# Cross attention's first two score steps, the output tiles and the first two pages' parts, each moved to an earlier place in a hybrid decoder step

## What is computed

```python
x = x + mix_output(o_gla, r, o_mla, lp)                    # w_out
x = x + cross_attend(rms_norm(x, lp['g_x']), mk, mv, lp)
x = x + ffn(rms_norm(x, lp['g_ff']), lp)

# latent attention of the prompt: causal softmax over the prompt's own keys, 8 heads
s = jnp.einsum('bthd,bshd->bhts', qn, kn) + jnp.einsum('bthd,bsd->bhts', qp, kp)
# latent attention of the samples: over 16 pages of 128 latent rows for each sequence
ckv = pool_ckv[pages]; kp = pool_kpe[pages]
kn, v = mla_decompress(ckv, lp)
# cross attention
q = rms_norm((h @ lp['w_xq']).reshape(B, T, X_HEADS, X_DIM), lp['g_xq'])
s = jnp.einsum('bthd,bnhd->bhtn', q, mk) * (X_DIM ** -0.5)
```

## Time and profile before

| | |
|---|---|
| median of 3 timed runs | 1205.99 us (1205.42 to 1207.26) |
| profiled execution, time | 1202.8 us |
| profiled execution, span | 1201.0 us |
| PE busy | 1153.9 us (96%) |
| VectorE, ScalarE, GpSimd busy | 607.1, 367.1, 310.3 us |
| mean granted clock of PE | 0.987 of full speed |
| read from memory | 107.90 MB |

### The profile page before, as it was taken

The page is one execution under the profiler, slowest core; times in us unless marked ns, Lnnn a source line. Parts: engine busy times, 40 slices in busy tenths (PEclk is TensorE's granted clock), DMA queues, the critical chain, the costliest instruction groups (busy, mean ns, idle before and its releaser), DMA issues.

```text
span 1201.0 us, 21983 instructions
## 1 busy us (share of the span) xinstructions
PE 1153.9 (96%) x8064; PEld 1022.8 (85%) x8064; DVE 607.1 (51%) x1062; ACT 367.1 (31%) x855; POOL 310.3 (26%) x180
## 2 busy tenths in 40 slices
PE   7999999989879999999989998999999999999997
PEld 4799896667869999999867764799999999999996
DVE  0659553767456677666621154444454444443442
ACT  4221124445444455545401143333310003330000
POOL 0127032720275777776602100300000000000000
PEclk9999999989999999999999999999999999999999
DMA  8432102100484444444126230222222222222102
GB/s 333 166 106 79 49 1 63 36 19 1 124 270 114 121 124 127 137 134 129 41 80 235 70 106 1 87 90 88 73 85 88 72 86 89 74 84 88 53 0 79
DMA packets 61601, 114.18 MB, mean 95 GB/s; under 512 B 6577, under 2 KB 41554, under 8 KB 61458
## 3 DMA queue, kind: packets, MB, share of 16 engines
q1 hardware_dynamic: 60946, 111.33, 29.7%
q0 software_dynamic: 576, 1.84, 0.4%
HBM read 107.90 MB, written 5.25 MB: 94 GB/s over the span
## 4 chain that ended last, share of the span: by engine, by line
PE 85%; DVE 4%; SPq 3%; issue 2%; POOL 2%; ACT 2%; DMA 2%; POOLq 0%; DVEq 0%; ACTq 0%
PE bank L1321 34%; PE bank L719 8%; PE bank L781 6%; PE bank L1133 5%; PE bank L1135 4%; PE bank L1134 4%; PE bank L799 3%; PE bank L743 2%; PE bank L1089 2%; PE bank L1160 2%; PE bank L1043 2%; PE bank L961 1%; SPq L629 1%; PE bank L1141 1%; PE bank L1063 1%
## 5 line engine op out<-in xcount | busy, mean ns | idle before, releaser
L1321 PE MATMUL bank<-hr,wr 128*128 128x288 f32 x1536 | 205.2, 296 | 1.0 <-DVEq L2295 1.0
L1321 PEld LDWEIGHTS bank<-hr,wr 128*128 128x128 f32 x1536 | 204.9, 189 | 1.4 <-issue 1.4
L1321 PE MATMUL bank<-ur,wr 128*128 128x288 f32 x1536 | 205.3, 296 | 0.0
L1321 PEld LDWEIGHTS bank<-ur,wr 128*128 128x128 f32 x1536 | 205.0, 189 | 0.1
L2609 POOL TENSOR_TENSOR stat<-stat,cst 128x32 f32<-128x32 f32 x32 | 175.2, 5476 | 2.5
L1133 PE MATMUL bank<-wq_high,c_parts 128*128 128x288 f32 x512 | 158.0, 309 | 2.6 <-DVE c_parts L2164 2.6
L1135 PE MATMUL bank<-wq_low,c_parts 128*128 128x288 f32 x512 | 152.6, 298 | 0.0
L1134 PE MATMUL bank<-wq_high,c_parts 128*128 128x288 f32 x512 | 151.7, 296 | 0.0
L2399 DVE CAST wr<-ring 128x1024 fp32r<-128x1024 f32 x64 | 44.4, 694 | 209.0 <-PE bank L1321 208.3
L2172 DVE TENSOR_REDUCE stat<-hT 128x8 f32<-128x512 f32 x128 | 86.6, 682 | 63.7 <-ACT hT L1633 61.7
L1133 PEld LDWEIGHTS bank<-wq_high,c_parts 128*128 128x128 f32 x512 | 97.3, 190 | 9.6 <-issue 8.4
(11 more groups left out here) (395 smaller groups left out, 1797.6 us busy)
## 6 DMA issues: line engine op xcount, KB each, us to landing
ring<-in_ring_w_dram SPq DMA_DIRECT2D x106, 512.0 KB, 3.6
arena<-in_page_rows_dram SPq DMA_DIRECT2D x128, 144.0 KB, 2.3
arena<-in_ckv_t_dram SPq DMA_DIRECT2D x96, 128.0 KB, 2.1
hT<-in_ckv_t_dram SPq DMA_DIRECT2D x32, 128.0 KB, 2.1
arena<-in_mk_t_dram SPq DMA_DIRECT2D x8, 512.0 KB, 3.2
arena<-in_cache_mv_dram SPq DMA_DIRECT2D x8, 512.0 KB, 10.2
mixT<-in_x_dram SPq DMA_DIRECT2D x1, 2048.0 KB, 12.9
out_dram<-hT SPq DMA_DIRECT2D x4, 512.0 KB, 3.2
```

The source lines that it names most:

```text
L1321: ins = mm(outs[c][:, 0:HALF], w[:, ew, k, :], src[:, ex, k0 + k, c * HALF:(c + 1) * HALF], start=(start and k == 0 and n == 0), stop=(sto ...
```

## The change

Four things are moved; no arithmetic is added or taken away.

1. In the query products PE does the third `value_rows` and the second `absorbed` before it waits for `q_ready` and `q_nope`, and `TURNED_ORDER`, ScalarE and VectorE follow this order.
2. The parts of the first pair of pages are made inside the prompt's attention: ScalarE's `high_parts(0, 0)` behind the third-last product with the values, VectorE's `turned(0, 0)` at the end of its steps. The buffer of the second pair of pages lies in `hT` now (column 512, over the second slot of `pr`), and SP loads this pair as soon as that slot has been turned the last time. PE no longer waits for the other engines at `phase_end`; it waits for the four banks of the page products, and for `page_one` only behind the first sequence.
3. SP issues the eight `W_OUT` tiles behind the first pair of pages, when `turned` is 4, and no longer behind the first `stream`.
4. In cross attention the first two score steps of the prompt stand behind the third query product, ahead of the fourth; the squares of the fourth query and the second roots come two steps later in the loop, and the banks of `cs` and `cp` are others.

```diff
     *(("kT", h) for h in range(4, MH)), ("vp", 0), "qTs", *(("kT", h) for h in range(4)), ("vp", 1), ("qabs", 0),
-    ("qT", 0), ("qT", 1), ("vp", 2), ("qabs", 1), ("qT", 2), ("qT", 3), ("qT", 4), ("qT", 5), "qpd", ("vp", 3),
+    ("vp", 2), ("qabs", 1), ("qT", 0), ("qT", 1), ("qT", 2), ("qT", 3), ("qT", 4), ("qT", 5), "qpd", ("vp", 3),
...
+    for b in range(2, 6):
+        fills[("page", b)] = (b, base[b])
...
-        fill(("cs", n % 4, n // 4), 1 + n % 2)
-        fill(("cp", n % 4, n // 4), 3 + n % 2)
+        fill(("cs", n % 4, n // 4), 2 + n % 2)
+        fill(("cp", n % 4, n // 4), (4, 1)[n % 2])
...
-        pages_t = [view(hT, 4096, 2, KC, P)] + [view(arena, c0, 2, KC, P) for c0 in (15908, 16420, 16932)]
+        pages_t = [view(hT, c0, 2, KC, P) for c0 in (4096, 512)] + [view(arena, c0, 2, KC, P) for c0 in (16420, 16932)]
...
 # SP
             sp.wait_ge(S("turned"), 4)
             load_pair(0, 0, 0)
+            for n in range(W_OUT, W_XQ):
+                load_tile(n)
+            b, n = PLAN[("pT", 3, MH - 3)]
+            sp.wait_ge(bank_full[b], n)
+            load_pair(0, 0, 1)
             sp.wait_ge(S("phase_end"), MET[3])
-            for n in range(1, 4):
+            for n in range(2, 4):
                 load_pair(0, 0, n)
             stream(0, 0, first=True)
-            for n in range(W_OUT, W_XQ):
-                load_tile(n)
...
 # PE
             absorbed(0)
+            value_rows(2)
+            absorbed(1)
             pe.wait_ge(S("q_ready"), TILES)
             pe.wait_ge(S("q_nope"), TILES)
-            for h in range(2):
-                turned_queries(h)
-            value_rows(2)
-            absorbed(1)
-            for h in range(2, 6):
+            for h in range(6):
                 turned_queries(h)
...
-            meet(pe, 3)
+            pe.drain().then_inc(S("phase_end"), 1)
...
+            for b in range(2, 6):
+                pe.wait_ge(bank_free[b], PLAN[("page", b)][1])
+            sequence(0, 0, first=True)
             pe.wait_ge(S("page_one"), 2)
-            sequence(0, 0, first=True)
...
                 project(("xq", j), lambda k: ring[:, s, k, :], hTk, KD, name=None if j else "x")
                 if j == 2:
                     query_squares(0)
+                    prompt_scores(0)
+                    prompt_scores(1)
...
-            for n in range(len(pairs) + 3):
+            for n in range(2, len(pairs) + 3):
                 if n < len(pairs):
-                    t, u = pairs[n]
...
+                    prompt_scores(n)
-                if n == 1:
+                if n == 3:
                     query_squares(1)
                 if n >= 3:
                     sample_scores(n - 3)
...
 # ScalarE
             for n in range(len(steps) + 5):
+                if n == len(steps) + 2:
+                    act.wait_ge(S("prT_used"), 4 * (MH // 2 - 1))
+                    high_parts(0, 0)
...
             def sequence(b, par, first=False, last=False):
-                if first:
-                    high_parts(b, 0)
...
+            for j in range(XH - 1):
+                query_squares(j)
...
                 if n == 1:
+                    query_squares(XH - 1)
+                if n == 3:
                     query_roots(1)
...
 # VectorE
             absorbed(0)
+            absorbed(1)
             turned_queries(1)
-            absorbed(1)
...
+            turned(0, 0)
             meet(dve, 3)
...
-                    if n in (0, 3):
-                        query_roots(n // 3)
+                    if n in (0, 4):
+                        query_roots(n // 4)
...
+                if n == 1:
+                    gained_queries(XH - 1)
```

More of the change, by code:

```diff
@@ L1209, in query_squares, with prompt_scores @@
                 filled(ins, ("ms_xq", u))
+            pairs = [(t, u) for u in range(2) for t in range(4)]
+            def prompt_scores(n):
+                t, u = pairs[n]
+                pe.wait_ge(S("xq"), 4 * u + 4)
+                o = reopen(pe, ("cs", t, u))
+                for e in range(2):
+                    h = 2 * u + e
+                    ins = mm(o[:, e * NM:(e + 1) * NM], xqT[:, h, t * P:(t + 1) * P], kmT[:, :, h, :],
+                             start=True, stop=True)
+                filled(ins, ("cs", t, u))
             for j in range(XH):
@@ L1215, in _ @@
                     query_squares(0)
-            pairs = [(t, u) for u in range(2) for t in range(4)]
+                    prompt_scores(0)
+                    prompt_scores(1)
             def sample_scores(q):
@@ L1590, in _, with high_parts @@
             arrive(act)
+            def high_parts(b, n):
+                act.wait_ge(S(f"page_t{n % 4}"), b * 128 + 64 * (n // 4 + 1))
+                if not (isinstance(b, int) and b == 0 and n < 2):
+                    act.wait_ge(S("kr"), b * NPG + (2 * n - 2))
+                nc.scalar.copy(c_parts[:, n % 2, 0, :, :, :].rearrange("p e k c -> p (e k c)"),
+                               pages_t[n % 4].rearrange("p e k c -> p (e k c)")).then_inc(S("c_high"), 1)
             steps = [(t, h) for t in range(4) for h in range(MH)]
             for n in range(len(steps) + 5):
+                if n == len(steps) + 2:
+                    act.wait_ge(S("prT_used"), 4 * (MH // 2 - 1))
+                    high_parts(0, 0)
                 if 3 <= n < len(steps) + 3 and (n - 3) % 2 == 1:
@@ L1634, in page_out @@
                   ACT.Square).then_inc(S("kr_free"), 1)
-            def high_parts(b, n):
-                act.wait_ge(S(f"page_t{n % 4}"), b * 128 + 64 * (n // 4 + 1))
-                if not (isinstance(b, int) and b == 0 and n < 2):
-                    act.wait_ge(S("kr"), b * NPG + (2 * n - 2))
-                nc.scalar.copy(c_parts[:, n % 2, 0, :, :, :].rearrange("p e k c -> p (e k c)"),
-                               pages_t[n % 4].rearrange("p e k c -> p (e k c)")).then_inc(S("c_high"), 1)
             def rope_keys(b, u):
@@ L1687, in _, with query_squares @@
                   scale=(EPS * XD / D) ** 0.5).then_inc(S("squares"), 1)
-            for j in range(XH):
+            def query_squares(j):
                 for c in range(2):
@@ L2129, in _, with turned @@
             dve.wait_ge(S("q_ready"), TILES)
+            def turned(b, n):
+                dve.wait_ge(S("c_high"), b * 8 + (n + 1))
+                V.tensor_tensor(c_parts[:, n % 2, 1, :, :, :].rearrange("p e k c -> p (e k c)"),
+                                pages_t[n % 4].rearrange("p e k c -> p (e k c)"),
+                                c_parts[:, n % 2, 0, :, :, :].rearrange("p e k c -> p (e k c)"),
+                                ALU.subtract).then_inc(S("c_low"), 1)
             steps = [(t, h) for t in range(4) for h in range(MH)]
@@ L2159, in _ @@
                 dve.nop().then_inc(S("sc_room"), 1)
-            def turned(b, n):
-                dve.wait_ge(S("c_high"), b * 8 + (n + 1))
-                V.tensor_tensor(c_parts[:, n % 2, 1, :, :, :].rearrange("p e k c -> p (e k c)"),
-                                pages_t[n % 4].rearrange("p e k c -> p (e k c)"),
-                                c_parts[:, n % 2, 0, :, :, :].rearrange("p e k c -> p (e k c)"),
-                                ALU.subtract).then_inc(S("c_low"), 1)
             def page_sums(b, j):
@@ L2247, in sequence @@
             def sequence(b, par, first=False, last=False):
-                if first:
-                    turned(b, 0)
                 for n in range(8):
@@ L2315, in _, with gained_queries @@
             add_to_x("wo", "x_mix", [(j, 0) for j in range(4)] + [(j, 1) for j in range(4)] + in_turn[8:], gained)
-            for j in range(XH):
+            def gained_queries(j):
                 for c in range(2):
@@ L2322, in _ @@
                     dve.wait_ge(S("xq"), n)
+            for j in range(XH - 1):
+                gained_queries(j)
             def query_roots(u):
```

9 lines of the change are left out of this document (1 added, 8 removed).

## The result

The changed kernel takes 1186.68 us (median of four runs, 1183.99 to 1190.21) against 1206.03 us before: a ratio of 0.984, with a 95% interval of 0.9813 to 0.9867. A later set of five runs gave 1188.82 us (1184.67 to 1190.79) against 1205.26 us, a ratio of 0.9871 (0.985 to 0.9892). The forecast was 1188.3 us.

The account below looks back on a forecast made before the run. The prediction took the matrix engine (PE), 85% of the chain, as the bound, through its waits and half-clock stretches. 5.62 + 3.36 + 8.35 + 0.4 = 17.7 us off the 1205.99 us median gave 1188.3 us, range 1185 to 1193.

Parts of the forecast that it names:

- Place A: Query products: a value and an absorbed product fill PE's 3.13 us wait, and the half clock behind it goes; gain 5.62 us.
- Place B: Hand-over from the prompt's attention to the pages: early parts and second pair put everything behind one pair earlier; gain 3.36 us.
- Place C: Output tiles: second sequence's pages no longer stand behind them on SP's queue; gain 8.35 us, bounds 6.66 to 8.35.
- Place D: Cross attention: two of ScalarE's steps run beside the fourth query product; gain 0.4 us, bounds -1.80 to 4.16.
- Rival 1: Clock falls at the hand-over and cross attention loses 1.80 us instead of winning 0.4: 1191.6 us; chance 0.20.
- Rivals 2 and 3: 2: half of Place C stays, 1192.5 us, chance 0.06; 3: most of Place B fails, A keeps half clock, 1194.2, 0.05.
- Rival 4: Attention: tiles hold six instruction transfers, 4.8 us each; attention 29 us longer, kernel at 1217 us; chance 0.03.

## Why the prediction was right

**Place A** was forecast at 5.62 us, its upper bound, and measured a little above it, at 5.80 and 5.74. The mechanism, idle time plus the half clock behind it, held; nobody held PE at the banks. The size is that of the one execution from which it was read. Over the four profiled executions with the old order the stage took 17.46 to 18.71 us, 17.99 on the mean, over the ten with the new order 12.95: the wait cost the same each time, the half clock behind it 1.4 to 2.6 us, and place A is worth 5.0 us on the mean.

**Place B** was forecast at 3.36 us and measured at 3.39 and 3.44. PE's first page product came 0.98 us after its last attention product, where some 0.7 us had been said, and the last release was the output copy, as said. One statement was off without touching the sum: PE was to wait for the third pair's transfer, and it reached the pair with less than 0.1 us to spare. The start itself was right: 309.93 is 8.61 us behind the start of the last product with the values, where the second pair had been 8.67 us behind. The early cast cost nothing: it ran while PE's last turning still did, the copy behind it starts 0.69 us after that turning (300.59 and 299.90), and PE waits 0.77 us for the copy, both as before.

**Place C** was forecast at 8.35 us. By the same spacing it measured 18.63 - 10.54 = 8.09 us. The spacing was read 0.26 us too small: 10.28 us had been taken one sequence on, and the second sequence keeps 10.54 us, of which 0.20 us is PE's wait for ScalarE ahead of `weighted`. By the whole stage it was 8.54 and 8.43 us, and 8.17 us alone. Here too the wait that goes is not a constant: the four profiled executions with all tiles at the old place had 6.66, 4.62, 6.37 and 7.61 us. Their stage took 49.41 us on the mean, the nine with all tiles early 40.91: 8.5 us. With four tiles the wait of 1.36 us follows from the bytes.

**Place D** was forecast at 0.4 us within -1.80 and 4.16. Eleven executions give 0.3 us on the mean, and 0.6 to 0.7 us at equal clock. The queue order that was to give most of the gain back did so, step by step: the second turning behind the sums of squares, then the roots, then VectorE. The run with the late second pair shows it, whose granted clock was 1.00 from there to 712 us: counted from the stage's start, ScalarE's fourth, fifth and sixth steps came 2.05, 1.02 and 0.65 us earlier than before, where 1.84, 0.86 and 0.4 us had been forecast. Three things were missing from the forecast. PE fell to half clock in the short products there in five of six executions; that 0.6 us less this loss comes so near to 0.4 us is luck. VectorE's product of the third step was held by GpSimd's addition (see the last section). And the step that holds the second turning has two causes: PE's order and VectorE's division, which stands behind the third step's maximum; taking away PE's order alone (the turning first) won nothing.

**The sum** of 17.7 us was 17.2 and 17.3 us by the stages, and 17.4 us by the means over all executions that hold a part whole or not at all (5.0, 3.6, 8.5 and 0.3): place A was 0.6 us smaller, B and C were a little larger. The median of the timed runs fell by 19.4 us in the first set and by 16.4 us in the second, so that 1186.68 us lies so near to 1188.3 us is in part luck too. Rival 1 named the half clock at the hand-over, which did not come (10.5 us for three pairs), and a loss in cross attention, which was at most 0.5 us. Rivals 2 and 3 did not happen. Rival 4, the slower one, was priced at 4.8 us for each held instruction transfer; three times the burst added none. What the forecast did not speak of is the spread: where the clock falls ahead of the change, and at the end of the pages (241.50 or 243.44 us), moves single runs by up to 6 us.

## What to carry to other kernels

Price a wait of the matrix engine with the half-clock stretch behind it: here that was 1.4 to 2.6 us on top of 3.13 to 3.15, 1.8 to 2.5 on top of 4.62 to 7.61, and 2.8 on top of 3.30. It is a range, so read it from more than one execution. Starting an engine earlier paid here only with its second operand early too; without the early second pair the hand-over became longer than before the change. Where run-to-run spread is as large as the part in question, compare the stage in several traces, and look at where in it the granted clock falls, before giving the part a sign.

## What the runs showed of the hardware that was not expected

The first 237 us hold the same instructions in all fourteen profiled executions, and took from 234.38 to 240.06 us. In the four longest (239.40 to 240.06) the mean granted clock of the first 234 us was 0.96 or 0.97, in the others 0.98 or 0.99; these still spread from 234.38 to 238.94 us, for a reason that no run here shows.

PE falls to half clock behind waits, and also behind hardly any. The granted clock was low after waits of 2.28 us (0.60 in the window 308 to 312 of the kernel before), 3.13 us and 3.30 us (0.53), and stayed at 1.00 after 0.98 us at the hand-over and 1.36 us with half the tiles. The length of the wait does not settle it: with the turning first, 1.35 us were followed by 0.58 (695 to 699 us). And in cross attention of the changed kernel it was 0.57 from 695 to 699 us after a wait of only 0.53 us, with PE busy for 4.00 of 4.00 us.

VectorE's product of 128x2 elements takes 0.16 us elsewhere in stage D, and took 0.96 to 0.97 us in the third step, while GpSimd added 128x576 elements, in all nine executions with place D; in the five without it, where that addition is over by then, it took 0.16 us. ScalarE's third step waited for it. VectorE's and GpSimd's timelines of the changed kernel:

```profile
692.86 0.97 DVE L2388 TENSOR_TENSOR stat<-stat 128x2 f32<-128x2 f32 x1
```

```profile
692.42 1.40 POOL L2654 TENSOR_TENSOR mixT<-mixT,rstd 128x576 f32<-128x576 f32 x1 [9.53 <-ACT mixT L1706]
```

VectorE's instruction ended at 693.83, as GpSimd's did (693.82). The Trainium skill (SBUF — State Buffer, "SBUF: two separate sides") says that the two share a pair of ports, which a GpSimd instruction, or a VectorE instruction with two inputs in SBUF against a GpSimd instruction that reads SBUF, holds to its end while the other blocks; these rows agree.
